# A seven-product form for the first matrix product of the second MLP, with its weight sums made by accumulating DMAs

## The reference

```python
def _sq_relu_mlp(h, w1, w2):            # w1: 1024 x 4096, w2: 4096 x 1024
    return jnp.square(jax.nn.relu(h @ w1)) @ w2
...
h_lat = h_lat + g2 * _sq_relu_mlp(_modulate(_rms_norm(h_lat, norm2_g[i]), sh2, sc2), mlp_w1[i], mlp_w2[i])
```

## Time and profile before

| what | value |
|---|---|
| median of 3 runs | 2430.54 us (2429.8 to 2430.73) |
| profiled execution, span of its instructions | 2428.1 us |
| PE busy | 2281.3 us (94%) |
| DVE busy | 1736.5 us (72%) |
| ACT, POOL busy | 1100.7, 1022.5 us |

### The profile page before, as it was taken

The page is one execution under the profiler, slowest core; times in us unless marked ns, Lnnn a source line. Parts: engine busy times, 40 slices in busy tenths (PEclk is TensorE's granted clock), DMA queues, the critical chain, the costliest instruction groups (busy, mean ns, idle before and its releaser), DMA issues. The chain is left out here.

```text
span 2428.1 us, 36937 instructions
## 1 busy us (share of the span) xinstructions
PE 2281.3 (94%) x11598; PEld 1900.3 (78%) x11598; DVE 1736.5 (72%) x2835; ACT 1100.7 (45%) x1985; POOL 1022.5 (42%) x816
## 2 busy tenths in 40 slices
PE   5989979999999999999699799888999999999998
PEld 3768868888888888888687677766778888888887
DVE  5653787777777777777774688871688787878776
ACT  5553443333333333333443588882343444444443
POOL 0003623433333443333656476765435353545443
PEclk9999999999999999999799899999999999999999
DMA  7434112222222222222212211104111111121212
GB/s 272 176 130 174 66 35 70 86 87 72 84 78 69 70 82 98 69 80 88 105 53 109 81 36 34 35 22 191 44 35 53 51 46 57 37 67 35 69 35 96
DMA packets 79297, 192.75 MB, mean 79 GB/s; under 512 B 6896, under 2 KB 15472, under 8 KB 75888
## 3 DMA queue, kind: packets, MB, share of 16 engines
q1 hardware_dynamic: 76288, 184.92, 22.4%
q10 hardware_dynamic: 2928, 6.82, 0.8%
HBM read 174.94 MB, written 16.78 MB: 79 GB/s over the span
## 5 line engine op out<-in xcount | busy, mean ns | idle before, releaser
L862 POOL TENSOR_TENSOR ht<-ht,l_side 128x512 f32<-128x512 f32 x224 | 301.3, 1345 | 919.2 <-ACT l_side L971 910.8
L1275 DVE SCALAR_TENSOR_TENSOR ht<-l_yy_ps,mod,ht 128x512 f32<-128x512 f32 x672 | 466.1, 743 | 26.9 <-PE l_yy_ps L1591 26.0
L51 PE MATMUL l_z_ps<-nh,l_w1h 128*128 128x512 f32 (+1 forms) x1280 | 474.2, 370 | 11.7 <-DVE nl L1215 6.3
L52 PE MATMUL l_z_ps<-nl,l_w1h 128*128 128x512 f32 (+1 forms) x1280 | 473.2, 370 | 0.0
L53 PE MATMUL l_z_ps<-nh,l_w1l 128*128 128x512 f32 (+1 forms) x1280 | 472.6, 369 | 0.0
L1589 PE MATMUL l_yy_ps<-l_ah,l_w2h 128*128 128x512 f32 x896 | 355.6, 397 | 9.8 <-DVE ht L1275 6.9
L1590 PE MATMUL l_yy_ps<-l_al,l_w2h 128*128 128x512 f32 x896 | 351.0, 392 | 0.0
L1591 PE MATMUL l_yy_ps<-l_ah,l_w2l 128*128 128x512 f32 x896 | 350.5, 391 | 0.0
L971 ACT ACTIVATE l_side<-l_yy_ps,mod 128x512 f32<-128x512 f32 x224 | 154.1, 688 | 335.2 <-PE l_yy_ps L1591 335.2
L51 PEld LDWEIGHTS l_z_ps<-nh,l_w1h 128*128 128x128 f32 x1280 | 242.4, 189 | 54.5 <-issue 7.6
L53 PEld LDWEIGHTS l_z_ps<-nh,l_w1l 128*128 128x128 f32 x1280 | 242.5, 189 | 40.7
(11 more groups left out here) (250 smaller groups left out, 4515.5 us busy)
## 6 DMA issues: line engine op xcount, KB each, us to landing
l_aw<-ada SPq DMA_DIRECT2D x128, 256.0 KB, 2.9
l_w1f<-w SPq DMA_DIRECT2D x64, 512.0 KB, 3.5
l_w2f<-w SPq DMA_DIRECT2D x64, 512.0 KB, 4.9
maw<-ada SPq DMA_DIRECT2D x24, 1024.0 KB, 5.3
queries<-qhl SPq DMA_DIRECT2D x16, 512.0 KB, 2.8
stage<-queries SPq DMA_DIRECT2D x32, 256.0 KB, 2.7
early<-fnet_w SPq DMA_DIRECT2D x11, 512.0 KB, 4.5
early<-wo SPq DMA_DIRECT2D x11, 512.0 KB, 3.5
```

The lines of the kernel that those rows point to most:

```text
L51: pe.matmul(out, lh, rh, start=first, stop=False)
L52: pe.matmul(out, lh, rl, start=False, stop=False)
L862: pool.tensor_tensor(h, h, side[(i - 1) % 2][:], ALU.add).then_inc(s_add, 1)
L1275: dve.scalar_tensor_tensor(out=h, in0=y_ps[m][:], scalar=mod[:, layer, G2, c, 0:1], in1=h, op0=ALU.mult, op1=ALU.add).then_inc(s_acc, 1)
```

## The change

Layer 1 gets a function of its own, `strassen_tail`. Its first two pairs form the four inner blocks by plain products. From the third pair on the first product is also seven block products of 4 k-steps each, in the order `Z_ORDER`, summed partly in PSUM; ACT copies three partial results to SBUF and DVE adds them (`zsum`). It needs four sums of token blocks, made once in pair 1 (`third_sum`, `first_sum`, `second_sum`, `fourth_sum`, four instructions each, and their high and low parts), and sums of w1. All weight sums of layer 1, for w1 and w2, are made in DRAM during layer 0: per pair SP issues four DRAM-to-DRAM copies (`start_sums`) and POOL four accumulating DMAs (`first_sums`, `more_sums`), 512 KB each. DVE's weight sums and one of its four low parts of w2 go. Most squared blocks stay in PSUM. The order of the seven second products is now M1, M6, M7, M4, M5, M3, M2. DVE's order after the inner blocks is `last_sums`. `load1` now loads halves of 256 KB from `w1` or from `sums`. The first pieces of `wo` are now loaded before w1 and w2.

```diff
+        s_sums = [ctx.enter_context(nc.semaphore(n)) for n in ("sums13", "sums2", "sums4")]
...
-        layer_tail(nc, sem, sb, banks, 1, wo, early, s_pw, w1, w2, mod, meanw, eps, ident, nh, nl, ht, park=park, out=out)
+        strassen_tail(nc, sem, sb, banks, wo, early, s_pw, w1, w2, sums, mod, meanw, eps, ident, nh, nl, nl_at, ht, park, out)
...
+                def start_sums(p):
+                    one, two = (slice(p, p + 1), slice(2 * p, 2 * p + 1)) if type(p) is int else (bass.ds(p, 1), bass.ds(p * 2, 1))
+                    to = slice(p + 1, p + 2) if type(p) is int else bass.ds(p + 1, 1)
+                    chunks = slice(2 * p, 2 * p + 2) if type(p) is int else bass.ds(p * 2, 2)
+                    if type(p) is not int or p:
+                        sp.wait_ge(s_s1, p * 32)
+                    sp.dma_start(sums[0, 0:2, to].rearrange("s a p n -> p (s a) n"), w1[1, one, :, :, 0:KC // 2].rearrange("a c p k n -> p (a c) (k n)")).then_inc(s_sc, 16)
+                    sp.dma_start(sums[0, 2:4, to].rearrange("s a p n -> p (s a) n"), w1[1, one, 0].rearrange("a p (h k) n -> p (a h) (k n)", h=2)).then_inc(s_sc, 16)
+                    sp.dma_start(sums[1, 0:2, to].rearrange("s a p n -> p (s a) n"), w2[1, two, :, :].rearrange("a p (d n) -> p (a d) n", d=2)).then_inc(s_sc, 16)
+                    sp.dma_start(sums[1, 2:4, to].rearrange("s a p n -> p (s a) n"), w2[1, chunks, :, 0:512].rearrange("c p n -> p c n")).then_inc(s_sc, 16)
                 def pair(r, row, rows, first):
+                    if C:
+                        start_sums(r)
...
+                def first_sums(p):
+                    one, to = (slice(p, p + 1), slice(p + 1, p + 2)) if type(p) is int else (bass.ds(p, 1), bass.ds(p + 1, 1))
+                    chunks = slice(2 * p, 2 * p + 2) if type(p) is int else bass.ds(p * 2, 2)
+                    pool.wait_ge(s_sc, p * 64 + 64)
+                    pool.dma_start(sums[0, 0:2, to].rearrange("s a p n -> p (s a) n"), w1[1, one, 1].rearrange("a p (h k) n -> p (a h) (k n)", h=2), accum_op=ALU.add, max_dma_last_dim=2048).then_inc(s_s1, 16)
+                    pool.dma_start(sums[1, 0:2, to].rearrange("s a p n -> p (s a) n"), w2[1, chunks, :, 512:1024].rearrange("c p n -> p c n"), accum_op=ALU.add, max_dma_last_dim=2048).then_inc(s_s1, 16)
+                def more_sums(p, name):
+                    to = slice(p + 1, p + 2) if type(p) is int else bass.ds(p + 1, 1)
+                    if name == "S2":
+                        pool.wait_ge(s_s1, p * 32 + 32)
+                    else:
+                        pool.wait_ge(s_s2, p * 16 + 16)
+                        if type(p) is not int or p:
+                            pool.wait_ge(s_s4, p * 16)
+                    dst, src = (2, 1) if name == "S2" else (3, 2)
+                    pool.dma_start(sums[:, dst, to].rearrange("w a p n -> p (w a) n"), sums[:, src, to].rearrange("w a p n -> p (w a) n"),
+                                   accum_op=ALU.add, max_dma_last_dim=2048).then_inc(s_s2 if name == "S2" else s_s4, 16)
                 def outputs(p, more):
                     add(p, "M5")
                     low2(p, "S2")
                     add(p, "M3")
+                    if C:
+                        first_sums(p)
                     if more and C:
                         low1(p + 1, 0)
                     low2(p, "S3")
                     for prod in ROWS[2:]:
                         add(p, prod)
+                        if C and prod in ("M2", "M7"):
+                            more_sums(p, "S2" if prod == "M2" else "S4")
...
+                    pool.wait_ge(s_s4, 16 * PAIRS)
...
+    PLAIN = 2
...
+    BANK = {"B21": 0, "B11": 1, "B12": 2, "B22": 3}
+    Z_ORDER = ["M1", "M5", "M6", "M2", "M7", "M3", "M4"]
+    Z_BANK = {"M1": 0, "M6": 0, "M7": 0, "M4": 0, "M2": 1, "M5": 2, "M3": 2}
+    Z_STARTS = ("M1", "M2", "M5")
+    W1_ORDER = ["A11", "S1", "S2", "A12", "S3", "S4", "A22"]
+    W1_PLAIN = ["A11", "A12", "A21", "A22"]
...
+    TOK_OF = {"M1": "B11", "M2": "B21", "M5": "T1", "M6": "T2", "M3": "B22", "M7": "T3", "M4": "T4"}
+    COPIES = ["M1", "M5", "M6"]
...
+    Y_ORDER = ["M1", "M6", "M7", "M4", "M5", "M3", "M2"]
+    Y_STARTS = ("M1", "M5", "M2")
+    INTO = {"M5": (1, 1), "M3": (0, 1), "M2": (0, 0), "M1": (0, 0), "M6": (0, 1), "M7": (1, 1), "M4": (1, 0)}
+    W2_ORDER = ["A11", "S2", "S3", "A22", "S1", "S4", "A12"]
...
+    HOME_BANK = {"B21": 0, "B11": 1, "T4": 1, "T3": 2, "B22": 3}
+    HOME_SLOT = {"T1": 0, "B12": 1, "T2": 3}
+    RELU_SLOT = {"B11": 0, "B12": 1, "B22": 2, "B21": 2}
+    SUM_AT = {"S3": 0, "S1": 1, "S2": 2, "S4": 3}
...
+                for w in range(2, RING_P + 2):
+                    load_p(w)
+                for i in range(4):
+                    load2(0, i)
...
+                def rest(p, more):
+                    if more:
+                        low1(p + 1, 0)
+                    low2(p, 3)
+                    add(p, 0)
+                    low2(p, 4)
+                    add(p, 1)
+                    low2(p, 5)
+                    add(p, 2)
+                    low2(p, 6)
...
+                def rest(p, more):
+                    relu(p, "B21")
+                    high(p, "T2")
+                    high(p, "T3")
+                    if more:
+                        high1(p + 1, 0)
+                    high(p, "T1")
+                    side_read(p, 0)
+                    high2(p, 3)
+                    high(p, "T4")
+                    high(p, "B22")
+                    side_read(p, 1)
+                    high2(p, 4)
+                    high(p, "B21")
+                    side_read(p, 2)
+                    high2(p, 5)
+                    side_read(p, 3)
+                    high2(p, 6)
...
+                def zsum(p, name):
+                    prod, part, k = {"B11": ("M2", "M1", 0), "B12": ("M3", "M6", 1), "B22": ("M7", "M5", 2)}[name]
+                    dve.wait_ge(s_z, z_at(p, prod))
+                    dve.wait_ge(s_cp, copied_at(p, part))
+                    to = slot[1][:] if name == "B12" else z_ps[BANK[name]][:]
+                    dve.tensor_tensor(to, z_ps[Z_BANK[prod]][:], slot[k][:], ALU.add).then_inc(s_x3, 1)
...
+                def last_sums(p, side_sums):
+                    diff(p, "T2")
+                    diff(p, "T3")
+                    low(p, "T2")
+                    low(p, "T3")
+                    acc(p, 0, 0)
+                    acc(p, 0, 1)
+                    if not (type(p) is int and p == 0):
+                        square(p, "B21")
+                    diff(p, "T4")
+                    low(p, "T1")
+                    acc(p, 0, 2)
+                    low(p, "T4")
+                    acc(p, 1, 0)
+                    low(p, "B22")
+                    acc(p, 1, 1)
+                    acc(p, 1, 2)
+                    acc(p, 2, 0)
+                    low(p, "B21")
+                    acc(p, 2, 1)
+                    acc(p, 2, 2)
+                    for i in (3, 4, 5, 6):
+                        for m in range(3):
+                            acc(p, i, m)
+                        if side_sums and i < 5:
+                            for j in range(HK):
+                                low_t("T1" if i == 3 else "T3", j)
...
+                def pair(p):
+                    for i in (0, 1, 2):
+                        low2(p, i)
+                    zsum(p, "B11")
+                    square(p, "B11")
+                    low(p, "B11")
+                    zsum(p, "B22")
+                    square(p, "B22")
+                    zsum(p, "B12")
+                    square(p, "B12")
+                    diff(p, "T1")
+                    last_sums(p, False)
...
+                for one in (third_sum, first_sum, second_sum, fourth_sum):
+                    for j in range(HK):
+                        one(j)
+                square(1, "B12")
+                diff(1, "T1")
+                square(1, "B22")
+                for j in range(HK):
+                    low_t("T4", j)
+                last_sums(1, True)
...
+                def hidden(p, prod):
+                    i = Z_ORDER.index(prod)
+                    pe.wait_ge(s_w1l, w1_at(p, i))
+                    if prod == "M1":
+                        pe.wait_ge(s_al, p * 7 + PRE)
+                    elif prod in ("M3", "M6", "M7"):
+                        pe.wait_ge(s_cp, copied_at(p, {"M6": "M1", "M3": "M5", "M7": "M6"}[prod]))
+                    elif prod == "M4":
+                        pe.wait_ge(s_x3, zsum_at(p, "B22"))
+                    name = TOK_OF[prod]
+                    start, end = prod in Z_STARTS, Z_BANK[prod]
+                    for j in range(HK):
+                        (wh, wl), (th, tl) = (w1h[:, i % 3, j], w1l[:, i % 3, j]), tokens(name, j)
+                        dst = z_ps[Z_BANK[prod]][:]
+                        if name == "T4":
+                            dst = wide(dst)
```

(32 more changed lines are left out.)

774 lines of the change are left out of this document (770 added, 4 removed).

## The result

The changed kernel takes 2570.2 us (2568.2 to 2572.5, four runs) against 2430.2 us (2429.5 to 2430.7): 1.057 times the time before, 95% interval 1.056 to 1.059, or 140 us more. The forecast was 2470 us, with 2438 to 2532 as range. The sign was right, the size was not: 40 us expected, 140 measured.

The account below looks back on a forecast made before the run. PE, busy 94% of the span, was taken to bound the kernel, with DVE close behind. The terms 12.3 + 9.5 - 0.5 - 1.3 + 18 + 1 = 39 us on a 2428.1 us span gave 2470 us, range 2438 to 2532.

Parts of the forecast that it names:

- DVE's row of thirteen: Layer-1 loop: thirteen DVE instructions in a row take at least 8.6 us, while PE has 6.8 us of matmuls.
- The DVE chain: Layer-1 loop after M3: PE waits for DVE of 0.6, 2.0 and 0.5 us, 3.1 us a pair with DVE undisturbed.
- Layer 0, +18 forecast: Layer 0: POOL's low parts come 1.0 to 1.1 us late at context group 2, +18 us over 16 pairs.
- The two move 1 MB: Layer 0: a pair's first two accumulations take 5.3 us like a 1024 KB load, so POOL's wait is nothing.
- the 1.85 us: Layer 0: cover between POOL's low parts of A22 and A21 (854.76) and PE's context group 2 (856.61).
- The loop, +12.3 forecast: Layer 1, pairs 3 to 16: waits of 3.6 us a pair, 50.4, against 38.1 us of matmuls saved.
- POOL's contention: Layer-1 loop: POOL slows DVE instructions with two SBUF inputs, taken as 0.5 us a pair.
- The +4 us that I gave for the rule on low T1: Layer-1 loop: if low T1 waits for POOL's whole instruction, up to 1.3 us, the term grows by 4 us.
- the clock rival: Layer-1 loop: waits drop PE to half rate in each pair, 14 x 1.4 = +20 us, 2490 us; chance 0.15.
- Second pair, +9.5: Layer 1, pair 2: 16 token sums and 12 low parts added on DVE make PE wait, +9.5 us (7 to 14).
- The start, -1.8: Layer 1, start and pair 1: M1 first gives -0.5 us, earlier loads of wo give -1.3 us.
- Layer 0 is the bound: Rival, layer 0: slow accumulations or shared DMA engines make POOL's low A21 5 us late, +80, 2530 us; chance 0.12.

Follow-up runs that it names:

- x9: Changed kernel, in layer 1's pairs 3 to 16 POOL starts its fifth w1 low part after square B12 and fourth w2 one after low T1: 2533.8 us.
- x8: Changed kernel with POOL's three DMAs of a pair in place but as plain copies of the same bytes, not accumulating: 2495.5 us.
- x10: Changed kernel, accumulations behind POOL's last add, copies behind `l_aw` loads (last pair's first two unmoved), M1's accs before low T3, two POOL waits: 2474.0 us.
- x11: Kernel before, with layer 1 loading three pieces of wo ahead of the first w1 and w2 blocks: 2430.6 us against 2431.4.
- x13: `x10` with the accs of M1 back in the changed kernel's order: 2466.8 us.
- x14: `x13` with POOL making pair 2's four low parts of T2's tokens behind its last add of the pair: 2468.4 us.
- x15: `x14` with DVE's row behind M3 spread, accs placed between low parts and squares: 2465.6 us.

## Why the prediction was wrong, point by point

**Right.** The sign; that layer 1's saved matmuls would be eaten by DVE's row of thirteen; the place of the waits in the loops (m=0 and m=2 of M6, context group 2 in layer 0); that copies cost nothing; 168 matmuls a pair. The DVE chain itself was nearly exact: without POOL beside it the sum was 38.2 + 3.1 = 41.3 us a pair, and `x9` has 41.6, with 2.1 us of waits and 1.3 us in small delays at other groups. The agreement is in the sum; the parts were 0.6, 2.0 and 0.5 and are 0.67, 1.42 and 0.13.

**Layer 0, +18 forecast, +75 measured, the step that failed most.** The step was "The two move 1 MB: 5.3 us if they are like a 1024 KB load"; they landed 8.0 us after the second issue (median of the second), and POOL went on after 8.65. I had the other end (10.6) in the text and chose the low one by an argument from the earlier trace rows about DRAM as a target, which holds for plain copies (`x8`: 4.6 us for the second) and says nothing about accumulating. With 8.65 us after a second issue at 846.4, my own sum gives a wait of 2.3 us where I had none, and 2.25 were seen. As in my sum, nothing covers what goes beyond the 1.85 us, so it counts in every pair. Two things lay outside the sum: that the load which follows POOL's low part comes late and is slower beside the accumulations (1.4 us a pair), and the slower starts of PE behind the wait (about 1.3 us in the pair shown). The Trainium skill (DMA: Bandwidth & Descriptors, Anatomy of one DMA — SWDGE (gpsimd) path), with which I had compared 5.3 us, gives a fixed cost and a rate for such a DMA, from which I had the estimate of 4.4 us for the two. The plain ones agree (4.6 us from the second issue in `x8`); the accumulating ones, at 8.0, do not.

**The loop, +12.3 forecast, +45.7 measured.** The mis-sized term is POOL's contention: 0.5 us a pair, measured 1.1 us on square B12 and 0.9 on low T1; the clock, below, is a term the sum had at nothing. I took a mean for two instructions that meet POOL by chance; in this loop of fixed order they meet it in every pair. (A third, the last of DVE's low parts of w2, takes 1.37 us in every loop pair, but in the first product, where PE does not wait.) Square B12 stood in none of my rows as a form with all its operands in SBUF. In the earlier trace rows the only row that did meet POOL, at 1.40 us, was the better guide than the mean of the earlier trace rows. The Trainium skill (SBUF — State Buffer, Who interferes with whom) says that the blocked instruction waits for the whole other one. The rows agree roughly: square B12 began 0.04 us after POOL's 1.29 us instruction and took 1.80, that is about 1.1 more; low T1 began 0.22 us after POOL's and took 0.9 more. Taken for both instructions the term would have been 2 us a pair. The +4 us that I gave for the rule on low T1 was also mis-added: 1.3 in place of 0.5 us in 14 pairs is +11.

**The clock.** I had it as a rival, for itself, at 1.4 us a pair. It is no rival but an addition: it came once contention made the waits longer. `x10` prices one fall at 1.7 us. In the changed kernel's pair above the seven starts behind the second wait take 3.15 us, where seven at full rate take 1.6: about 1.5 of the 2.8 us by which this pair is longer than one of `x9`. In layer 0, where I had not asked for it, it is the 1.3 us told above.

**Second pair, +9.5 and +17.6.** The 16 token sums took what was forecast (10.4 us, against 16 x 0.67 = 10.7). The low parts did not: four of T4 5.97 us and four of T1 6.2 us instead of 2.7, beside POOL's; the four of T3, with POOL idle, took 2.5. The same error as in the loop. The place was off too: I had the wait on the third acc, and 6.25 us of it stand on the first and 1.09 on the third.

**The start, -1.8 and -7.2.** The gain was there and larger; the reason I gave for part of it, the order of the loads, is refuted by `x11`.

**The chances.** "Layer 0 is the bound", 2530 us, had 0.12, and the clock rival 0.15. They were not exclusive, and both came about in the main, with contention on top; the range took each alone and so ended at 2532, 38 us short.

With the repairs found, `x13` still pays 11 us in layer 0 (6 to 10 in `x10`, `x14` and `x15`), 8 in the loop and 17 in the second pair, has 5 back from the stretch up to it, and is 1.5% slower than the kernel before. No version run here beats the kernel before.
